# Modulation sums of two transformer blocks: the fold over partitions, on VectorE and in one small product, in place of eight turns on TensorE

## The reference, cut to what matters

```python
c_act = jax.nn.silu(c)                       # (1, 1024)
mod = c_act @ w_ada[l] + b_ada[l]            # (1, 6144): six vectors of 1024
sh1, sc1, g1, sh2, sc2, g2 = [m[:, None, :] for m in jnp.split(mod, N_MOD, axis=-1)]
h = rmsnorm(x, norm1_g[l]) * (1.0 + sc1) + sh1
...                                          # attention, pooling: mix
x = x + g1 * mix
h2 = rmsnorm(x, norm2_g[l]) * (1.0 + sc2) + sh2
x = x + g2 * conv_gated_ffn(h2, w_up[l], conv_w[l], conv_b[l], w_down[l])
```

## Time and profile before

| what | value |
|---|---|
| three runs | 1463.28, 1467.45, 1469.25 us (median 1467.45) |
| profiled execution | 1463.28 us, span 1463.3 us |
| busy share of the span | PE 96%, DVE 57%, POOL 48%, ACT 45% |
| attention loop of the first block | up to about 210 us of the span |
| its first feed-forward network | about 240 to 640 us |
| mean granted TensorE clock | 0.983 of full speed |

### The profile page before, as it was taken

One profiled execution on the slowest core, in us unless ns is written; L12 is line 12 of the kernel. 1 busy time (PEld: TensorE's weight loads), 2 busy tenths in 40 slices (PEclk: granted clock), 3 DMA queues, 4 the chain that ended last, 5 costly groups with the idle time before them and its releaser, 6 DMA issues.

```text
span 1463.3 us, 18686 instructions
## 1 busy us (share of the span) xinstructions
PE 1406.7 (96%) x7447; PEld 1187.9 (81%) x7447; DVE 833.2 (57%) x1300; ACT 655.4 (45%) x1202; POOL 704.5 (48%) x377
## 2 busy tenths in 40 slices
PE   7789989999999999999999999999999999999997
PEld 7668778988888888887877877888898888888886
DVE  5567746677878675646777975644366311213125
ACT  4455536434332332634777764456454332323232
POOL 1246554455554553653333453348806655646440
PEclk7899999999999999999999999999999999999998
DMA  9525532365556464321222221114301232232311
GB/s 328 132 65 163 178 108 99 111 205 183 181 186 221 164 200 153 112 83 58 58 58 71 74 58 58 58 58 152 108 30 58 90 112 86 98 104 87 115 58 58
DMA packets 141767, 167.62 MB, mean 115 GB/s; under 512 B 14192, under 2 KB 125424, under 8 KB 141680
## 3 DMA queue, kind: packets, MB, share of 16 engines
q1 hardware_dynamic: 141680, 166.42, 35.7%
HBM read 164.31 MB, written 2.10 MB: 114 GB/s over the span
## 4 chain that ended last, share of the span: by engine, by line
PE 83%; DVE 8%; ACT 4%; POOL 2%; issue 1%; DMA 1%; SPq 0%; DVEq 0%; ACTq 0%
PE B L550 80%; PE B L972 1%; POOL WL L2241 1%; ACT WH L1156 1%; DVE SC L1899 1%; PE B L782 1%; DVE SC L2127 1%; DVE ZF L2102 1%; PE B L665 1%; DMA RAW<-in_x 1%; POOL G L2279 0%; DVE M L2100 0%; DVE ZF L2082 0%; DVE SC L1716 0%; PE B L688 0%
## 5 line engine op out<-in xcount | busy, mean ns | idle before, releaser
L2241 POOL TENSOR_TENSOR WL<-RAW,WH 128x512 fp32r<-128x512 f32 (+1 forms) x196 | 476.9, 2447 | 520.3 <-ACT WH L1156 475.0
L550 PE MATMUL B<-HH,WH 128*128 128x512 f32 (+2 forms) x1040 | 404.1, 391 | 6.0 <-ACT HH L1242 2.1
L550 PE MATMUL B<-HH,WL 128*128 128x512 f32 (+2 forms) x1040 | 397.1, 384 | 0.0
L550 PE MATMUL B<-HL,WH 128*128 128x512 f32 (+2 forms) x1040 | 385.6, 383 | 0.0
L550 PE MATMUL B<-ZR,WH 128*128 128x512 f32 (+1 forms) x1200 | 326.0, 359 | 0.1
L1156 ACT ACTIVATE WH<-RAW 128x512 fp32r<-128x512 f32 (+1 forms) x196 | 195.3, 1026 | 193.7 <-PE B L550 185.6
L550 PEld LDWEIGHTS B<-ZR,WH 128*128 128x128 f32 x1200 | 214.4, 189 | 33.4 <-POOL WL L2241 0.3
L550 PEld LDWEIGHTS B<-HH,WH 128*128 128x128 f32 x1040 | 196.7, 189 | 46.1 <-issue 4.3
L550 PEld LDWEIGHTS B<-HH,WL 128*128 128x128 f32 x1040 | 196.4, 189 | 39.0
L550 PEld LDWEIGHTS B<-HL,WH 128*128 128x128 f32 x1040 | 191.8, 189 | 34.3
L550 PE MATMUL B<-ZR,WL 128*128 128x512 f32 (+1 forms) x600 | 214.8, 358 | 0.0
(11 more groups left out here) (230 smaller groups left out, 1647.9 us busy)
## 6 DMA issues: line engine op xcount, KB each, us to landing
ZF<-in_w_ada SPq DMA_DIRECT2D x84, 512.0 KB, 4.5
RAW<-in_w_ff SPq DMA_DIRECT2D x32, 1024.0 KB, 5.3
RAW<-in_w_up SPq DMA_DIRECT2D x22, 1024.0 KB, 5.1
RAW<-in_w_in SPq DMA_DIRECT2D x16, 1024.0 KB, 5.0
RAW<-in_w_in SPq DMA_DIRECT2D x19, 512.0 KB, 5.1
RAW<-in_w_down SPq DMA_DIRECT2D x8, 1024.0 KB, 5.5
G<-in_w_ada SPq DMA_DIRECT2D x8, 512.0 KB, 10.2
RAW<-in_w_out SPq DMA_DIRECT2D x4, 1024.0 KB, 5.0
```

Of the source, the lines that this page charges most:

```text
L550: return e.matmul(out, l, r, start=start, stop=stop)
L2241: e.tensor_tensor(lo[:, at], k.RAW[:, i % 2, at], hi[:, at].bitcast(F32), ALU.subtract).then_inc(*w.hit((i, q)))
```

## The change

For the nine vectors 3 to 11 VectorE does more of the sum itself. `ada_fold(j)` turns the accumulator in blocks of 32 x 32 (one instruction of 128 x 1024 into `G[:, 0:1024]`), then reduces each turned block along its row, so that 128 x 1024 becomes 128 x 32. Within each quarter of 32 partitions this is the sum over that quarter. PE's `ada_sum(j)` is then one fp32 product with a constant 128 x 128 matrix (1 where two indices agree modulo 32) and 32 moving columns, into one PSUM bank. VectorE adds the bias with four small operations, one for each quarter of the partitions. The vectors 0 and 1 keep the old way.

The constant is loaded by a DMA of its own in step 20, over a constant (`BD`) that is no longer needed by then. For the vectors 5 to 11 the fold follows the eighth chunk at once. The folds of the vectors 4 and 3, in this order, stand in VectorE's step 32, ahead of `ada_mod(2)` and of step 33; they write to G and wait for `("pool", 3)`.

```diff
+        self.FOLD = self.BD
...
     def ada_sum(j, rings=("main", "main")):
+        if j > 1:
+            b = B.take(pe, rings[0], ("ada", j))
+            pe.wait_ge(k.sig("in_fold")[0])
+            pe.wait_ge(v_ada["part", j])
+            mm(b[:, 0:32], k.FOLD, k.ACC[j % 2][:, 0:32], True, True).then_inc(*ada_full.hit(("sum", j)))
+            return
...
             if j > 2:
-                dve.wait_ge(ada_full["sum", {3: 1, 4: 0}.get(j, j - 2), 1])
+                dve.wait_ge(ada_full["sum", {3: 1, 4: 0}[j], 1] if j < 5 else ada_full["sum", j - 2])
...
+        if kt == 7 and j > 4:
+            ada_fold(j)
+
+    def ada_fold(j):
+        turned, dst = k.G[:, 0:1024], k.ACC[j % 2]
+        dve.wait_ge(ada[j, 7])
+        dve.wait_ge(g_mix["pool", 3])
+        if j != 4:
+            dve.wait_ge(ada["part", {3: 4, 5: 3}.get(j, j - 1)])
+        e.transpose(turned, dst).then_inc(*ada.hit(("turned", j)))
+        dve.wait_ge(ada["turned", j])
+        e.tensor_reduce(dst[:, 0:32], turned.rearrange("p (b n) -> p b n", b=32), AX, ALU.add).then_inc(*ada.hit(("part", j)))
...
     def ada_mod(j):
...
+        if j > 1:
+            dve.wait_ge(ada_full["sum", j])
+            for i in range(4):
+                at = slice(32 * i, 32 * i + 32)
+                e.tensor_tensor(k.MOD[at, j, :], B["ada", j][at, 0:32].rearrange("p (f i) -> p f i", i=4)[:, :, i], bias[at, :],
+                                ALU.add).then_inc(*ada.hit(("mod", j)))
+            B.free(("ada", j), ada["mod", j])
+            return
...
             rotated(SCALED[s - 1], *QKS[SCALED[s - 1]][:2])
+        if s == 32:
+            ada_fold(4)
+            ada_fold(3)
         ada_point(("1", s))
...
+        if s == 20:
+            sp.wait_ge(k.sig("pe_head")["q3"])
+            load("in_fold", 0, k.FOLD, a["consts"][:, 2624:2752])
```

More of the change, by code:

```diff
@@ L55, in constants @@
     return np.ascontiguousarray(np.concatenate(
-        [ident, bd, caus, stneg, edge, cos1, sin1, cos2, sin2], axis=1).astype(f))
+        [ident, bd, caus, stneg, edge, cos1, sin1, cos2, sin2, i[:, None] % 32 == i[None, :] % 32], axis=1).astype(f))
 def vectors(a):
```

## The result

The changed kernel takes 1470.89 us (median of 15 runs, 1468.39 to 1472.67), the kernel before in the same session 1467.45 us (15 runs, 1463.28 to 1470.60). The ratio is 1.0022 with a 95% interval of 1.0014 to 1.0029: about 3.3 us slower (3.2 by the ratio, 3.4 between the medians), resolved by the runs, yet within the 0.5% that the prediction called "same". The forecast was +2.4 us.

The account below looks back on a forecast made before the run. PE, busy without a gap in the feed-forward network, was taken as the bound. Span 1463.3 + 5.2 (stall) + 1.8 (clock) - 0.6 - 4.0 (sums) = 1465.7, 2.4 more; on the median 1469.9 us, range 1463 to 1477.

Parts of the forecast that it names:

- same: Whole kernel: a time within 0.5%, 7.3 us, of the kernel before; given chance 0.80, slower 0.14, faster 0.06.
- The step that decided: Step 33: vector 4's product waits for a ring `t` bank freed by `lo`, behind both folds and `ada_mod(2)`; 5.2 us.
- stall of PE: Step 33: PE, ready at 198.03, stands until 203.2, 5.2 us (3.0 to 7.6), with nothing to absorb it.
- clock behind it: After the step 33 wait: PE's granted clock falls to half, costing 1.8 us (bounds 0 and 2.0).
- vector 4's sum: End of the attention loop: the 32-column product in place of eight turns saves 0.6 us.
- sums in the network: Feed-forward network: seven sums on PE's path save 0.57 us each, 4.0 us in all (2.9 to 5.3).
- some 3: Sign of being right: after PE's wait near 198, some 3 us at half clock.
- Vector 3's saving: Ahead of the projection's last tiles, which wait for VectorE and ScalarE anyway: 0 us, up to 0.6 and 0.8 more.
- Turn and reduction: VectorE's fold: turn 1.30 us and reduction 1.22, with waits 2.6 us a fold (1.5 to 3.8).
- (a): Step 33: PE waits only for fold 4, 1.8 us, too short to lower the clock; 1464.7 us; chance 0.16.
- (b): Network: folds held by GpSimd, weight slabs late, deciding from about 4.5 us per fold; 11 us more, 1481; chance 0.10.
- (c): Network: PE's gain given back, as slab splits pace it or the 32-column product costs as much as turns; 1474; chance 0.08.

Follow-up runs that it names:

- experiment 1: Changed kernel with the folds of vectors 4 and 3 behind `lo` in step 33 and vector 4's sum moved to step 36: 1462.73 us, 0.9976 of before.
- exp. 5: Changed kernel with the folds of vectors 4 and 3 behind `lo` in step 33, vector 4's sum left in step 33: 1466.60 us, 0.9997 of before.
- exp. 6: Changed kernel with vector 4's product taking its bank from ring `s` and vector 2's bias ahead of the two folds: 1467.29 us, 0.9997 of before.
- experiment 11: From experiment 1: six dummy fp32 products in PE's 3.14 us wait ahead of the pooling branch's mean: 1463.36 us, 0.9970 of before.
- experiment 10: From exp. 5: three dummy fp32 products of 512 columns ahead of PE's wait for fold 4: 1466.51 us, 0.9989 of before.
- exp. 3: Changed kernel folding only vectors 4 and 3, the vectors 5 to 11 in the old way with eight turns: 1473.36 us, 1.0049 of before.
- exp. 4: Changed kernel with vector 4's product taking its bank from ring `s` instead of ring `t`: 1469.82 us, 1.0018 of before.
- exp. 7: Changed kernel with fold 4 left in step 32 and fold 3 moved to step 33 behind `lo`: 1467.15 us, 0.9998 of before.
- experiment 2: Changed kernel folding only vectors 5 to 11, the vectors 4 and 3 in the old way with eight turns: 1462.37 us, 0.9969 of before.
- experiment 12: From exp. 5: two dummy fp32 products of 512 columns ahead of PE's wait for fold 4: 1465.18 us, 0.9993 of before.
- experiment 9: From experiment 1: turn and reduction of vectors 5 to 11 each run twice, 5.0 us a fold: 1464.47 us, 0.9974 of before.
- experiment 8: From experiment 1: turn and reduction of vectors 5 to 11 each run three times, 7.4 us a fold: 1476.70 us, 1.0068 of before.

## Why the prediction was right, and where its steps were off

**The step that decided was right.** PE's product waits for the bank of ring `t`, that for the first half of `lo`, that for both folds and vector 2's bias, these for `("pool", 3)`. The stall came out at 4.9 us (198.39, when PE was ready, to 203.32) and not 5.2, mostly since a fold is 2.51 us and not 2.6. Experiments 1, 5 and 6 show it by cause: with the folds behind `lo`, or the banks free, what is left is the wait for fold 4 (1.66 us), and none with the sum three steps later. Term by term, against the traces:

| term | forecast | traces |
|---|---|---|
| stall of PE | +5.2 | +4.9 |
| clock behind it | +1.8 | +2.8 |
| vector 4's sum | -0.6 | -0.3 |
| sums in the network | -4.0 (seven) | -3.8 (six) |
| together | +2.4 | +3.6 |

Vector 4's saving is small because its product ran at half clock: the next one starts 0.45 us behind it, where the eight turns took 0.79.

**The clock was the mis-sized term: 1.8 us, bound 2.0, measured 2.8.** From 203.77 to 227.25 PE does in 23.48 us what took it 20.67 before (198.82 to 219.49). Two steps were off. The 1.8 was read too high for its own wait: it set 4.28 us for the 24 products against 3.04, but behind products of 512 columns they take 3.43 at full clock too (the earlier trace rows at 174.45, experiment 11 at 191.34). From the start of the first to the next turns it is 5.18 us before (187.91 to 193.09) and 3.73 at full clock in experiment 11, so that wait cost 1.45 us. And I had carried it over to the new wait, behind which PE works at half clock for 6.5 us and not "some 3". The profile by windows shows where the half clock begins and ends. The loss is the time from the product of vector 4 to that of vector 3 less the 22.6 us of experiment 10, which ran at full clock:

| kernel | idle ahead of it | at half clock | of that, behind the wait | lost |
|---|---|---|---|---|
| the change | 4.77 us | 199.6 to 209.8 | 6.5 us | 3.1 us |
| exp. 3 (only 4 and 3) | 4.76 | 198.8 to 205.6 | 3.2 | 1.6 |
| exp. 4 (other ring; less its second wait, 1.91) | 1.66 | 201.6 to 208.4 | 4.4 | 2.3 |
| exp. 5 | 1.66 | 201.8 to 208.6 | 6.4 | 3.0 |
| exp. 6 | 1.66 | 199.9 to 206.8 | 6.1 | 2.9 |
| exp. 7 | 2.22 | 200.2 to 203.6 | 3.4 | 1.7 |

The loss is about half of the time that PE works at half clock; the part of the half clock that falls into the wait costs nothing. So it does not grow with the wait: 4.8 us of idle time gave 3.1 once and 1.6 once, because in experiment 3 the clock was back at 205.6, as its windows show (columns as above):

```profile
198.00:199.00 1.00, 0.00 (x0) 0.88 0.99 217
205.00:206.00 1.00, 1.00 (x4) 0.71 0.05 16
```

Each row of the table is one execution, and what decides how long the clock stays down is not shown.

**The sums: 0.64 us each in place of 0.57.** The next product starts 0.14 us behind the 32-column product (209.13 and 209.27 in experiment 1) and 0.79 behind the eight turns. These are six sums. The seventh, vector 11's, saves 0.66 at its place, but soon behind it PE comes to wait for GpSimd's WL (at 610.68, the same product at 606.81 before): the shift is +3.90 us at the sum and +3.87 there, so all of the saving but 0.03 is lost. The prediction counted seven. The timed network half, -4.5 us (-6.0 to -2.9), agrees with six (-3.8) as well as with seven.

**Vector 3's saving was put at 0**, and is 0 in the change's trace: the shift is +7.76 at its sum and +7.72 at the product with ONES, where PE now waits 3.04 us in place of 1.38. What the prediction missed is that this longer wait can cost clock. Behind it the clock stayed at 1.00 in the change's trace, but fell in those of all eleven other kernels that fold vector 3; in before and in experiment 2, which do not, the wait is 1.38 and 1.36 us and the clock stays. The product with ONES, in the change and then in experiment 1:

```profile
245.45 1.54 PE L551 MATMUL B<-SC,ONES 128*128 128x256 f32 x4 [3.04 <-DVE SC L1723]
```

```profile
236.64 2.07 PE L551 MATMUL B<-SC,ONES 128*128 128x256 f32 x4 [3.04 <-DVE SC L1723]
```

From it to vector 11's sum it is 358.4 us in the change and in experiment 2, and 359.4 to 359.9 in the experiments 1, 4 to 7 and 10 to 12: 1.0 to 1.5 us more. A kernel that folds 4 to 11 and leaves vector 3 as it was has not been run.

**Turn and reduction, 1.245 and 1.220 us**, for 1.30 and 1.22 worked out from the slope of the shorter ones. The estimate of 2.5 us for the turn from the 311 ns that the Trainium skill has ("VectorE: DVE Perf Modes", section "The three transpose paths") is not borne out: eight blocks of 128 x 128 in one instruction cost half of eight instructions by that figure. The measurement decides.

**What is missing from the prediction** is the second blocked bank (bank 1, experiment 4). It changed no number, since it comes free 0.6 us before the bank of ring `t`, but with it "the bank of ring `t`" is only half the reason: freeing that bank alone takes 1.2 us off the 4.8 of idle time.

**The rivals.** (a) fell twice: the change does wait for `lo`, and where only fold 4 is waited for (experiments 5 and 6), 1.66 us are not too short to lower the clock. The kernels then come out at before's time (0.9997), and not 2.8 us under it as (a) had it: the clock eats the sums' gain. (b) fell by the durations: all nine turns lie within 2 ns and all nine reductions too. The one at 361.29 runs beside GpSimd's split of a slab, and the reduction behind it too (362.57, 1.22 us); VectorE and then GpSimd after:

```profile
361.29 1.25 DVE L1827 STREAM_TRANSPOSE G<-ZF 128x1024 f32<-128x1024 f32 x1
```

```profile
360.37 5.38 POOL L2271 TENSOR_TENSOR WL<-RAW,WH 128x2048 fp32r<-128x2048 f32 x1 [0.20 <-ACT WH L1163]
```

By what the Trainium skill says of the second read interface ("VectorE: DVE Perf Modes", section "Two Vector instructions with no wait between them") neither should be held, and the trace agrees. The point from which (b) would decide was put at 4.5 us a fold; at 5.0 PE waits 0.8 us in all and the time cannot be told from experiment 1's, at 7.4 it costs 14 us, of which only the 4.0 at the slabs are of the kind that (b) describes. (c) fell with experiment 2: -4.5 us stay, though the last sum's gain is lost in the way of (c), to a wait for GpSimd's split.

**A faster kernel than either** is experiment 1, or experiment 2's network half; at 0.9976 and 0.9969 their intervals overlap, and the runs do not tell which is better.

## What to carry to other kernels

Work put into an engine's queue delays every buffer that is freed behind it: list all of them (here two banks, one for the product itself and one for the tile after it), and not only the result that the new work makes. A saving on the saturated engine counts where that engine never waits, and there it held to 0.1 us a piece; at the seams between stages (the sums of the vectors 11, 3 and 4) it counted nothing or was overpaid, because a PE that is sooner there waits longer, and a longer wait can lower its clock. A wait of under 2 us on PE can cost more in clock than in idle time, so moving the folds behind `lo` and their product three steps later was worth 7 to 8 us, and moving the folds alone 4.

## What the runs showed that I had not expected

- PE was at half clock for 6 us after a wait of 1.66 us (with one of 0.93 shortly before it), and dummy products in the wait kept it at 1.00.
- The same wait has not always the same price. The 2.46 us wait for GpSimd's ZR at about 650 us is in all 14 traces, in code that no kernel here alters. In 5 of them (before and the experiments 5, 6, 9 and 11) the clock stays at 1.00 behind it. In the other 9 it falls: within the twelve products (1.29 to 1.75 us in place of 1.15) in the change and the experiments 1, 2, 3, 7 and 10, and right behind them in the experiments 4, 8 and 12, where the twelve still take 1.15 or 1.16 us and the next products start 0.43 us apart, as here in experiment 4:

```profile
657.94 1.16 PE L551 MATMUL B<-ZR 64*128 64x256 f32 x12 [2.46 <-POOL ZR L2283]
659.03 0.79 PE L551 MATMUL B<-HH,WH 128*128 128x512 f32 x1
659.63 0.63 PE L551 MATMUL B<-HL,WH 128*128 128x512 f32 x1
```

  From this wait to the end of the span it is 809.7 to 810.5 us in the 5, and 811.2 to 811.6 in the 9. There is one trace of each kernel, so they do not show by themselves that it goes with the execution. The runs speak for it: of 29 executions of the kernel before in the session of the experiments 5 to 8, the shortest (span 1461.2 us) has a mean granted clock of 0.984 and the longest (1470.2) one of 0.977. What decides it stays open. It may be a part of the spread of the runs: those of experiment 1 lie in two groups, 1461.8 to 1462.7 and 1463.6 to 1464.4.
- An fp32 product of 512 columns takes 0.86 us of PE, as six records in 2.58 us show (two records a product). The 0.46 us from the start of such a product to that of the next operation at 174.45 was no price for it: its own row runs on to 175.01, over the products that follow, and these take 0.4 us more for it (3.43 in place of 3.04).
